# Attention rounds: the third value chunk's transposes, its eviction and the stores of the values moved to the next round's beginning

## The chip, the cores and the metric

The kernel runs on one core of a Trainium2 chip. The metric is the device time of one execution in microseconds (us); lower is better. A core has a matmul engine (TensorE, "PE" in the profile; its weight loads are "PEld"), a vector engine (VectorE, "DVE"), an activation engine (ScalarE, "ACT"), GpSimd ("POOL") and SyncE ("SP"). Each engine works through its own list of instructions in order, and the engines wait for each other by semaphores. DMAs are issued from the lists of SP and of ACT. Matmuls write PSUM, which has 8 banks; the other engines move results from there to SBUF.

## What is computed

The reference is one step of a four-layer decoder trunk for 1024 prompt positions and 8 sample rows, 1032 columns in all. Layer 1 is the one that matters here, differential attention with 8 heads:

```python
q, k, v, g = diff_project(hp, diff_w_in[j], diff_q_gain[j], diff_k_gain[j])
op = diff_output(diff_attend_prompt(q, k, v, lam), g, diff_sub_gain[j], lam_init, diff_w_out[j])
...
    s = jnp.einsum('bthmd,bshmd->bmhts', qb, k).astype(jnp.float32) * scale - slopes[:, None, None] * dist[None]
    s = jnp.where(dist >= 0, s, -jnp.inf)
    p = jax.nn.softmax(s, axis=-1)
    o = jnp.einsum('bmhts,bshv->bmhtv', p, vf)
    return jnp.moveaxis(o[:, 0] - lam * o[:, 1], 1, 2)
```

For the sample rows the same is done against a paged cache of 1024 past positions. The values v of the prompt and of the samples are outputs too (`v_rows_prompt`, `v_cols_sample`), and so are the keys (`k_cols`).

## The kernel before

Activations are held transposed, features by columns, and the 1032 columns are cut into three chunks of 384, 384 and 264 (`CHUNKS`). A weight block of 1024 x 128 is a *unit*; PE multiplies it with one chunk in `unit_chunk`, 8 k-tiles of 3 matmuls each (lines 284 to 286, high and low parts). ACT splits a unit's weights (`split_hi`, line 240) and POOL makes the low part (line 244).

Layer 1 is done in nine *rounds* (`diff_rounds`): round i projects head i (units q, k, v, and the gate g, which belongs to the next round's steps 0 to 2) and does the attention of head i − 1. Round 0 has no attention, round 8 no projection; rounds 1 to 7 are one loop body. On each engine a round is 12 steps s, written out by hand in `body`, and what comes after them. On PE a step puts the first half of a unit chunk (`ks=range(0, KT // 2)`), then attention work, then the second half. The attention works on 8 blocks of 128 query rows: `scores(t)` (line 1283), `probs(tb, half)`, which transposes the probabilities (line 1299), and `values(tb)`, which multiplies them with the values (line 1310). Between them DVE adds the bias and takes the maximum (line 1603), ACT takes exponentials (line 1534), and DVE combines the two softmaxes (lines 1613 to 1616); ACT moves the transposed probabilities to SBUF (line 1473).

Values come out of the projection with features along the partitions and must be turned. `unit_evac` copies a chunk of v from PSUM to `hraw` (line 1458); `value_chunk(x)` on PE transposes its blocks of 128 into a PSUM bank (line 1370); `value_evac(x)` on ACT copies them to `vf` (line 1466) and counts up the semaphore `d_rg`. Chunks 0 and 2 use the same bank (`RG`), and `value_chunk(2)` waits until `d_rg` tells that all evictions before it in the round are done. In the kernel before all this is done in the round of the projection: `value_chunk(0)` in step 10, `value_chunk(1)` in step 11, and behind the steps `value_chunk(2)`, after eight transposes of the finished attention output (line 1416) and ahead of the last small product of the sample rows (line 1423, for a root that ACT makes at lines 1549 and 1551). ACT's end of the round is: two evictions of the attention output (line 1541), `unit_evac(11)`, `value_evac(1)`, `value_evac(2)`, the root, and then DMAs: the attention output (line 1554), the values (lines 1560 and 1562), the keys (line 1565) and the sample output (line 1568). The next round begins on ACT with a load of an activation table (line 1489), `split_hi`, the exponentials of block 0, and the Tanh of the gate's chunk 0 (line 1444), with DVE's product at line 1626. The gate's chunks are stored from ACT's list in steps 2 to 4 (line 1527); the gate's chunk 2 uses chunk 0's buffer and waits for that store (`d_gst`). SP loads slabs of the paged keys and values, 512 KB each (line 1203), as PE frees their slots.

The first scores of a round wait for many things, the last eviction of the values among them:

```python
                    if t == 0:
                        pe.wait_ge(d_qk, done(r.p1.at(0)))
                        pe.wait_ge(d_or, prior(r.p2.at(0)))
                        pe.wait_ge(d_De, prior(r.p2.at(0)))
                        pe.wait_ge(d_rg, done(r.p9.at(8)))
```

`d_rg` counts nine evictions a round: six of the norms of q and k (line 1483) and three of the values, so `p9.at(8)` is the last value eviction of the previous round and `p9.at(7)` the one before it.

Of the kernel before, what the change touches and what calls it, by code (L numbers as in the profile page):

```python
# [15 lines left out]
P = 128  # L16
# [139 lines left out]
def trunk(nc, A, LAYERS=4):  # L156
    ctx = ExitStack()
    with ctx:
# [3 lines left out]
        def sem(name):  # L162
            return ctx.enter_context(nc.semaphore(name))
# [36 lines left out]
        unit_ev = sem("unit_ev")  # L200
# [11 lines left out]
        def ev_val(u, c):  # L212

            return u * NC_ + (c + 1 + CR)
# [375 lines left out]
        def prior(n):  # L590
            return n + 1

        def done(n):
            return n + 2
# [509 lines left out]
        vf = al.take(NBLK, DV)  # L1104
# [19 lines left out]
        wself, vsf, vws, osm, osq2, ors = (al.take(NS) for _ in range(6))  # L1124
# [12 lines left out]
        d_sqd, d_sm, d_rg, d_rq, d_t1 = (sem(x) for x in ("d_sqd", "d_sm", "d_rg", "d_rq", "d_t1"))  # L1137
# [14 lines left out]
        d_kst, d_vst, d_vss, d_sst = sem("d_kst"), sem("d_vst"), sem("d_vss"), sem("d_sst")  # L1152
# [115 lines left out]
        def diff_pe(pe):  # L1268
            def body(r):
                def scores(t):  # L1270
                    if t == 0:
                        pe.wait_ge(d_qk, done(r.p1.at(0)))
                        pe.wait_ge(d_or, prior(r.p2.at(0)))
                        pe.wait_ge(d_De, prior(r.p2.at(0)))
                        pe.wait_ge(d_rg, done(r.p9.at(8)))
                    if t == 4:
                        pe.wait_ge(d_ss, done(r.p1.at(0)))
                    pe.wait_ge(d_mx, prior(r.p16.at(2 * t)))
                    W = (t + 1) * P
                    for a in range(0, W, 512):  # L1280
                        e = min(W, a + 512)
                        for m in range(2):
                            last = nc.tensor.matmul(SSC[m][:, a:e], qf[64 * m:64 * m + 64, t * P:(t + 1) * P],  # L1283
                                                    kf[64 * m:64 * m + 64, a:e], start=True, stop=True)
                            if e == W:
                                last.then_inc(d_sc, 1)
# [16 lines left out]
                def values(tb):  # L1303

                    if r.proj and tb >= 2:
                        pe.wait_ge(d_rg, done(r.n9.at(tb - 2)))
                    pe.wait_ge(d_pe, done(r.p12.at(pidx(tb, tb // 4))))
                    pe.wait_ge(d_on, prior(r.p8.at(tb)))
                    for b in range(tb + 1):
                        last = nc.tensor.matmul(DOB[:, 0:P], pT[tb % 2][:, b, :], vf[:, b, :], start=(b == 0),  # L1310
                                                stop=(b == tb))
                    last.then_inc(d_o, 1)
# [45 lines left out]
                def value_chunk(x):  # L1358

                    c0 = CHUNKS[x][0]  # L1360
                    pe.wait_ge(unit_ev, ev_val(r.unit.at(2), x))
                    pe.wait_ge(d_rg, prior(r.n9.at(6 + x)) if x != 1 else prior(r.n9.at(6)))
                    if r.attn and x == 1:
                        pe.wait_ge(d_mx, done(r.p16.at(15)))
                    if r.attn and x == 0:
                        pe.wait_ge(d_on, done(r.p8.at(7)))
                    for b, w in blocks_of(x):
                        if b < NBLK:
                            o = b * P - c0
                            last = nc.tensor.transpose(VTR[x][:, o:o + P], hraw[:, x % 2, o:o + w], ident[:, :])  # L1370
                    last.then_inc(d_t1, 1)

                for s in range(12):
                    if (s >= 2 * NC_ if r.first else r.proj or s < NC_):
                        unit_chunk(pe, r.unit, s // NC_ - 1, s % NC_, FILL_AT[1], ks=range(0, KT // 2))
                    if r.attn and 3 <= s <= 10:
                        values(s - 3)
                    if r.attn and 2 <= s <= 9:
                        probs(s - 2, 0)
                    if r.attn and s < NBLK:  # L1380
                        scores(s)
                    for b in V_AT.get((s, 0), ()) if r.attn else ():
                        value_row(b)
                    if r.attn and s == 11:
                        pe.wait_ge(d_vo, done(r.p1.at(0)))
                        nc.tensor.matmul(OSB, vo, selv, start=True, stop=True).then_inc(d_vs, 1)
                    if r.attn and 6 <= s <= 9:
                        probs(s - 2, 1)
                    if (s >= 2 * NC_ if r.first else r.proj or s < NC_):
                        unit_chunk(pe, r.unit, s // NC_ - 1, s % NC_, FILL_AT[1], ks=range(KT // 2, KT))  # L1390
                    if r.attn and s in K_AT:
                        key_rows(K_AT[s])
                    if r.attn and s == 3:
                        self_keys()
                    for b in V_AT.get((s, 1), ()) if r.attn else ():
                        value_row(b)
                    if r.attn and s == 5:
                        sample_weights()
                    if r.first and s == 4:
                        pe.wait_ge(d_ld, 16 * 15)  # L1400
                    if r.proj and 4 <= s <= 9:
                        x = s - 4
                        c0, w = CHUNKS[x % NC_]
                        pe.wait_ge(d_sqd, done(r.n6.at(x)))
                        pe.wait_ge(d_rg, prior(r.n9.at(x)))
                        if r.attn:
                            pe.wait_ge(d_on, done(r.p8.at(s - 3)))
                        nc.tensor.matmul(RG[:, 0:w], blk, ss[:, c0:c0 + w], start=True, stop=True).then_inc(d_sm, 1)
                    if r.proj and s >= 10:
                        value_chunk(s - 10)  # L1410
                    if r.attn and s == 11:
                        pe.wait_ge(d_dn, done(r.p1.at(0)))
                        pe.wait_ge(d_pe, done(r.p12.at(11)))
                        for half in range(2):
                            for y in range(4):
                                last = nc.tensor.transpose(DB[half][:, y * P:(y + 1) * P], dall[:, 4 * half + y, :],
                                                           ident[:, :])
                            last.then_inc(d_D, 1)
                if r.proj:
                    value_chunk(2)  # L1420
                if r.attn:
                    pe.wait_ge(d_ssq, done(r.p1.at(0)))
                    nc.tensor.matmul(FSB, ones[:, :], osq2, start=True, stop=True).then_inc(d_F, 1)
# [4 lines left out]
        def diff_act(act):  # L1428
# [5 lines left out]
            def body(r):  # L1434
                i = r.i
# [24 lines left out]
                def value_evac(x):  # L1460
                    c0 = CHUNKS[x][0]
                    nb = 3 if x < 2 else 2
                    act.wait_ge(d_t1, done(r.n3.at(x)))
                    if x == 0:
                        act.wait_ge(d_vst, r.n1.at(0) * 16 + 16)
                    act.activation(vf.rearrange("p b d -> p (b d)")[:, c0:c0 + nb * P], VTR[x][:, 0:nb * P], ACT.Copy)\
                       .then_inc(d_rg, 1)
# [18 lines left out]

                for s in range(12):
                    if r.attn and s == 0:
                        act.preload_act_table_set("exp_and_others")
                    if (s > NC_ if r.first else r.proj or s <= NC_) and s >= 1:  # L1490
                        unit_evac(s - 1)
                    if s == 4:
# [36 lines left out]
                    if r.attn and s < NBLK:  # L1529
                        W = (s + 1) * P  # L1530
                        act.wait_ge(d_nm, done(r.p8.at(s)))
                        for m in range(2):
                            x = (S0[s % 3], S1[s % 2])[m][:, 0:W]
                            act.activation(x, x, ACT.Exp, bias=nm2[:, s % 2, m:m + 1],  # L1534
                                           accum_out=(l8[:, s:s + 1], l1[:, s % 2:s % 2 + 1])[m]).then_inc(d_ex, 1)
                    if r.proj and s == 11:
                        value_evac(0)
# [5 lines left out]
                if r.proj:  # L1543
                    unit_evac(11)
                    value_evac(1)
                    value_evac(2)
                if r.attn:
                    act.wait_ge(d_F, done(r.p1.at(0)))
                    act.activation(ors, FSB, ACT.Ln, bias=eps_t[:, 0:1], scale=1.0 / DV).then_inc(d_or, 1)
# [6 lines left out]
                                      dall[:, 4 * half:4 * half + 4, :].rearrange("p b t -> p (b t)"))\  # L1556
                           .then_inc(d_ost[half], 16)
                if r.proj:
                    act.wait_ge(d_rg, done(r.n9.at(8)))
                    act.dma_start(A["v_rows_prompt"][0, 0, :, bass.ds(i, 1), :]  # L1560
                                  .rearrange("(b p) a d -> p b (a d)", p=P), vf).then_inc(d_vst, 16)
                    act.dma_start(A["v_cols_sample"][bass.ds(i, 1), :, :].rearrange("a d b -> (a d) b"), vsf)\
                       .then_inc(d_vss, 16)
                    act.wait_ge(d_qk, done(r.n1.at(0)))
                    act.dma_start(A["k_cols"][bass.ds(i, 1), :, :].rearrange("a d t -> (a d) t"), kf).then_inc(d_kst, 16)
                if r.attn:
# [522 lines left out]
```

## Time and profile before

| what | value |
|---|---|
| three runs | 3464.18, 3462.76, 3458.08 us (median 3462.76) |
| the profiled execution: its own time | 3459.76 us |
| its span, first to last instruction | 3457.7 us |
| mean granted TensorE clock | 0.973 |
| busy share: PE, PEld, DVE, ACT, POOL | 92%, 82%, 39%, 34%, 15% |
| attention rounds 1 to 7, from one round's first scores to the next's | 91.20 to 93.70 us each |
| DMA | 450.65 MB, mean 130 GB/s |

The profile is of one execution. A busy time counts an engine's instructions, not its waits; ends of matmuls are modelled and matmuls overlap, so a busy PE isn't one at its peak. In the rows below a timeline line gives the start, the time taken, the engine (ACTq and SPq are DMA issues in the lists of ACT and SP), the line of the kernel and the operation with what it writes and reads, and in brackets the idle time of the engine before it and what ended that. Times in us are counted from the span's start.

### The profile page before, as it was taken

The numbers are of one execution on the slowest core, as the hardware profiler recorded it, in microseconds if no ns is written. First come the engines' busy times: TensorE is split into PE (matmuls) and PEld (weight loads), VectorE is DVE, ScalarE is ACT, GpSimd is POOL, SyncE is SP. The second block draws the span as 40 slices with busy tenths as digits, with TensorE's granted clock in tenths as the row PEclk, the third lists the DMA queues.
The fourth block names the chain that finished last, engine by engine and source line by source line (L and its number), as shares of the span: only waits on it lengthen the run. The fifth ranks groups of instructions, "written<-read, shape, count | busy, mean of one in ns | idle before, by whom it ended". The sixth has DMA issues, their size and how long they took to land.

```text
span 3457.7 us, 55121 instructions
## 1 busy us (share of the span) xinstructions
PE 3186.2 (92%) x19786; PEld 2825.5 (82%) x19786; DVE 1354.3 (39%) x3415; ACT 1176.0 (34%) x2293; POOL 523.6 (15%) x224
## 2 busy tenths in 40 slices
PE   6999999997998999999968899979799999999799
PEld 5979697986997777777758788869797979788699
DVE  3231414134434334344345666653524141423531
ACT  3232313232224444444433454531323231323320
POOL 1111020111111101101101122211111101111021
PEclk8999999999999999999989999989899999999999
DMA  6758484757214343444343122131133332424722
GB/s 181 245 156 262 131 244 163 230 186 243 67 37 143 120 137 123 136 137 136 133 144 120 38 60 59 59 113 43 43 120 123 106 129 74 151 87 138 242 76 74
DMA packets 530067, 450.65 MB, mean 130 GB/s; under 512 B 24978, under 2 KB 464658, under 8 KB 529874
## 3 DMA queue, kind: packets, MB, share of 16 engines
q1 hardware_dynamic: 423362, 325.77, 30.4%
q10 hardware_dynamic: 106512, 122.27, 10.2%
q8 instruction: 125, 2.05, 0.2%
q14 instruction: 68, 0.56, 0.0%
HBM read 348.58 MB, written 166.50 MB: 149 GB/s over the span
## 4 chain that ended last, share of the span: by engine, by line
PE 75%; DVE 10%; issue 5%; ACT 4%; DMA 3%; SPq 2%; POOL 1%; ACTq 0%; DVEq 0%; POOLq 0%
PE psum L284 19%; PE psum L285 18%; PE psum L286 18%; PE psum L898 3%; PE psum L894 3%; PE psum L1283 2%; PE psum L1310 2%; DVE Hl L324 2%; DVE hraw L368 2%; PE psum L890 2%; PE psum L873 1%; SPq L393 1%; DMA arena<-scratch_g 1%; POOL Wl L244 1%; PE psum L1353 1%
## 5 line engine op out<-in xcount | busy, mean ns | idle before, releaser
L284 PE MATMUL psum<-Hh,Wh 128*128 128x384 f32 (+1 forms) x4896 | 1646.2, 336 | 163.3 <-DVE Hl L324 64.3
L285 PE MATMUL psum<-Hl,Wh 128*128 128x384 f32 (+1 forms) x4896 | 1583.6, 323 | 0.0
L286 PE MATMUL psum<-Hh,Wl 128*128 128x384 f32 (+1 forms) x4896 | 1582.9, 323 | 0.0
L284 PEld LDWEIGHTS psum<-Hh,Wh 128*128 128x128 f32 x4896 | 938.6, 192 | 236.6 <-issue 99.4
L285 PEld LDWEIGHTS psum<-Hl,Wh 128*128 128x128 f32 x4896 | 940.7, 192 | 6.5 <-issue 0.9
L286 PEld LDWEIGHTS psum<-Hh,Wl 128*128 128x128 f32 x4896 | 938.0, 192 | 0.0
L244 POOL TENSOR_TENSOR Wl<-wraw,Wh 128x1024 fp32r<-128x1024 f32 (+1 forms) x208 | 495.0, 2380 | 2729.4 <-ACT Wh L240 2729.1
L240 ACT ACTIVATE Wh<-wraw 128x1024 fp32r<-128x1024 f32 (+1 forms) x208 | 215.8, 1038 | 339.5 <-PE psum L286 204.6
L419 DVE TENSOR_TENSOR xT<-psum,xT 128x384 f32<-128x384 f32 (+1 forms) x168 | 86.5, 515 | 358.9 <-PE psum L286 358.2
L317 ACT ACTIVATE Hh<-hraw 128x384 fp32r<-128x384 f32 (+1 forms) x252 | 116.2, 488 | 169.3 <-DVE hraw L411 98.7
L953 ACT ACTIVATE hraw<-psum 128x384 f32<-128x384 f32 (+1 forms) x96 | 44.1, 459 | 318.8 <-PE psum L286 318.8
L1052 DVE SCALAR_TENSOR_TENSOR arena<-arena,psum 128x512 f32<-128x512 f32 x56 | 41.9, 748 | 259.2 <-PE psum L898 259.2
L1534 ACT ACTIVATE arena<-arena 128x256 f32<-128x256 f32 (+7 forms) x128 | 98.2, 768 | 116.2 <-DVE arena L1607 116.2
L1074 DVE SCALAR_TENSOR_TENSOR arena<-arena 128x512 f32<-128x512 f32 x128 | 88.9, 747 | 109.7 <-ACT arena L988 109.7
L1040 DVE COPY arena<-psum 128x384 f32<-128x384 f32 (+1 forms) x96 | 48.6, 506 | 212.1 <-PE psum L873 212.1
L993 ACT ACTIVATE arena<-psum,arena 128x512 f32<-128x512 f32 x64 | 44.1, 689 | 248.1 <-DVE arena L574 248.1
L324 DVE TENSOR_TENSOR Hl<-hraw,Hh 128x384 fp32r<-128x384 f32 (+1 forms) x252 | 126.1, 537 | 2.8 <-ACT Hh L317 2.0
L898 PE MATMUL psum<-arena 128*128 128x512 f32 x256 | 120.3, 592 | 0.0
L1603 DVE CUSTOM_DVE_ANT_0 arena<-psum,arena 128x256 f32<-128x256 f32 (+7 forms) x128 | 92.4, 755 | 68.1 <-PE psum L1283 67.4
L1035 DVE TENSOR_SCALAR arena<-psum,arena 128x384 f32<-128x384 f32 (+1 forms) x48 | 27.6, 574 | 226.2 <-PE psum L873 226.2
L894 PE MATMUL psum<-arena 128*128 128x512 f32 x224 | 105.3, 592 | 0.0
L898 PEld LDWEIGHTS psum<-arena 128*128 128x128 f32 x256 | 48.6, 190 | 61.2 <-issue 61.2
(198 smaller groups left out, 2831.7 us busy)
## 6 DMA issues: line engine op xcount, KB each, us to landing
wraw<-in_ret_w_in SPq DMA_DIRECT2D x96, 512.0 KB, 4.2
scratch_kc<-in_cache_kt SPq DMA_DIRECT2D x64, 512.0 KB, 6.1
scratch_vc<-in_cache_vt SPq DMA_DIRECT2D x64, 512.0 KB, 6.7
arena<-in_state_ret ACTq DMA_DIRECT2D x64, 512.0 KB, 6.3
out_ret_state_sample<-arena ACTq DMA_DIRECT2D x64, 512.0 KB, 3.9
arena<-scratch_kc SPq DMA_DIRECT2D x64, 512.0 KB, 4.2
arena<-scratch_vc SPq DMA_DIRECT2D x64, 512.0 KB, 4.3
scratch_on<-arena ACTq DMA_DIRECT2D x80, 256.0 KB, 2.4
```

What stands on the lines that cost most here:

```text
L240: act.activation(Wh[:, j % 2, 0:kt * P], wraw[:, j % 2, 0:kt * P], ACT.Copy).then_inc(w_hi, 1)
L244: pool.tensor_tensor(Wl[:, j % 2, 0:kt * P], wraw[:, j % 2, 0:kt * P], Wh[:, j % 2, 0:kt * P].bitcast(F32), ALU.subtract).then_inc(w_lo, 1)
L284: nc.tensor.matmul(out, hi, xh, start=(k == 0), stop=False)
L285: nc.tensor.matmul(out, hi, xl, start=False, stop=False)
L286: last = nc.tensor.matmul(out, lo, xh, start=False, stop=(k == kt - 1))
L317: act.activation(Hh[:, k, c0:c0 + w], hraw[:, n % HR, 0:w], ACT.Copy).then_inc(h_hi, 1)
L324: nc.vector.tensor_tensor(Hl[:, k, c0:c0 + w], hraw[:, n % HR, 0:w], Hh[:, k, c0:c0 + w].bitcast(F32), ALU.subtract).then_inc(h_lo, 1)
L894: last = nc.tensor.matmul(OB[:, :], qdT[:, r % 2, x, :], St[:, x, :], start=False, stop=(x == 1))
L898: last = nc.tensor.matmul(sbk[:, :], ktok[:, r, x * P:(x + 1) * P], vtok[:, r, :], start=True, stop=True)
L1074: last = nc.vector.scalar_tensor_tensor(sring[:, b % 4, x, :], vbr[:, b % 4, :], kT[:, x, SEQ + b:SEQ + b + 1], sring[:, b % 4, x, :], ALU ...
L1534: act.activation(x, x, ACT.Exp, bias=nm2[:, s % 2, m:m + 1], accum_out=(l8[:, s:s + 1], l1[:, s % 2:s % 2 + 1])[m]).then_inc(d_ex, 1)
L1603: nc.vector.tensor_tensor_reduce(out=(S0[t % 3], S1[t % 2])[m][:, 0:W], in0=SSC[m][:, 0:W], in1=strip[:, SEQ - W:SEQ], scale=1.0, scalar=- ...
```

## The change

The transposes of the values' third chunk move on PE from behind the steps to step 0 of the next round, between the first half of its unit chunk and the scores of block 0. Their eviction on ACT moves to the beginning of the next round, ahead of the table load. The two DMAs that store the values move to step 1 of the next round on ACT, ahead of the first Tanh, and now take the index i − 1. The scores of block 0 wait for the second eviction of values in place of the third; step 3, ahead of the first product with values, waits for the third.

```diff
@@ -1272,7 +1272,7 @@
                         pe.wait_ge(d_qk, done(r.p1.at(0)))
                         pe.wait_ge(d_or, prior(r.p2.at(0)))
                         pe.wait_ge(d_De, prior(r.p2.at(0)))
-                        pe.wait_ge(d_rg, done(r.p9.at(8)))
+                        pe.wait_ge(d_rg, done(r.p9.at(7)))
                     if t == 4:
@@ -1358,8 +1358,12 @@
                 def value_chunk(x):
 
                     c0 = CHUNKS[x][0]
-                    pe.wait_ge(unit_ev, ev_val(r.unit.at(2), x))
-                    pe.wait_ge(d_rg, prior(r.n9.at(6 + x)) if x != 1 else prior(r.n9.at(6)))
+                    if x == 2:
+                        pe.wait_ge(unit_ev, ev_val(r.unit.at(-2), x))
+                        pe.wait_ge(d_rg, prior(r.p9.at(8)))
+                    else:
+                        pe.wait_ge(unit_ev, ev_val(r.unit.at(2), x))
+                        pe.wait_ge(d_rg, prior(r.n9.at(6)))
                     if r.attn and x == 1:
@@ -1373,7 +1377,11 @@
                 for s in range(12):
                     if (s >= 2 * NC_ if r.first else r.proj or s < NC_):
                         unit_chunk(pe, r.unit, s // NC_ - 1, s % NC_, FILL_AT[1], ks=range(0, KT // 2))
+                    if r.attn and s == 0:
+                        value_chunk(2)
                     if r.attn and 3 <= s <= 10:
+                        if s == 3:
+                            pe.wait_ge(d_rg, done(r.p9.at(8)))
                         values(s - 3)
@@ -1416,8 +1424,6 @@
                             last.then_inc(d_D, 1)
-                if r.proj:
-                    value_chunk(2)
                 if r.attn:
                     pe.wait_ge(d_ssq, done(r.p1.at(0)))
@@ -1460,7 +1466,7 @@
                 def value_evac(x):
                     c0 = CHUNKS[x][0]
                     nb = 3 if x < 2 else 2
-                    act.wait_ge(d_t1, done(r.n3.at(x)))
+                    act.wait_ge(d_t1, done(r.p3.at(x) if x == 2 else r.n3.at(x)))
@@ -1486,7 +1492,14 @@
                 for s in range(12):
                     if r.attn and s == 0:
+                        value_evac(2)
                         act.preload_act_table_set("exp_and_others")
+                    if r.attn and s == 1:
+                        act.wait_ge(d_rg, done(r.p9.at(8)))
+                        act.dma_start(A["v_rows_prompt"][0, 0, :, bass.ds(i - 1, 1), :]
+                                      .rearrange("(b p) a d -> p b (a d)", p=P), vf).then_inc(d_vst, 16)
+                        act.dma_start(A["v_cols_sample"][bass.ds(i - 1, 1), :, :].rearrange("a d b -> (a d) b"), vsf)\
+                           .then_inc(d_vss, 16)
@@ -1543,7 +1556,6 @@
                     unit_evac(11)
                     value_evac(1)
-                    value_evac(2)
@@ -1556,11 +1568,6 @@
                 if r.proj:
-                    act.wait_ge(d_rg, done(r.n9.at(8)))
-                    act.dma_start(A["v_rows_prompt"][0, 0, :, bass.ds(i, 1), :]
-                                  .rearrange("(b p) a d -> p b (a d)", p=P), vf).then_inc(d_vst, 16)
-                    act.dma_start(A["v_cols_sample"][bass.ds(i, 1), :, :].rearrange("a d b -> (a d) b"), vsf)\
-                       .then_inc(d_vss, 16)
                     act.wait_ge(d_qk, done(r.n1.at(0)))
```

The lines of the changed kernel stand 4 to 13 further down, so 1370 becomes 1374, 1423 becomes 1429, 1466 becomes 1472 and 1489 becomes 1496. PE's list at the end of the loop body of rounds 1 to 7, before: the transposes of the values' second chunk, eight of the attention output, then those of the third chunk, the sample product and the loop's branch.

```order
L1370 MATMUL psum<-ident,hraw 128x128 x2
L1416 MATMUL psum<-ident,arena 128x128 [waits d_pe,d_dn]
L1416 MATMUL psum<-ident,arena 128x128 x7
L1361 REGISTER_ALU
L1362 REGISTER_ALU [waits unit_ev]
L1370 MATMUL psum<-ident,hraw 128x128 [waits d_rg]
L1370 MATMUL psum<-ident,hraw 128x128
L1423 MATMUL psum<-arena,ones 128x8 [waits d_ssq]
L1185 REGISTER_ALU
L1185 COMPARE_AND_BRANCH
```

In the changed kernel the third chunk's transposes, with their waits for `unit_ev` and `d_rg`, are gone from there:

```order
L1374 MATMUL psum<-ident,hraw 128x128 x2
L1424 MATMUL psum<-ident,arena 128x128 [waits d_pe,d_dn]
L1424 MATMUL psum<-ident,arena 128x128 x7
L1429 MATMUL psum<-arena,ones 128x8 [waits d_ssq]
L1185 REGISTER_ALU
L1185 COMPARE_AND_BRANCH
```

They stand now on PE in step 0 of the next round, between the last matmuls of the unit chunk's first half and the scores of block 0 (line 1283):

```order
L284 MATMUL psum<-Hh,Wh 128x384
L285 MATMUL psum<-Hl,Wh 128x384
L286 MATMUL psum<-Hh,Wl 128x384
L1374 MATMUL psum<-ident,hraw 128x128 [waits d_rg,unit_ev]
L1374 MATMUL psum<-ident,hraw 128x128
L1283 MATMUL psum<-arena 128x128 [waits d_rg,d_De,d_mx,d_or,d_qk]
L1283 MATMUL psum<-arena 128x128
```

Nothing else moved on PE. On ACT the list from the loop's branch into the next pass was, before, the table load, the weights' split, the exponentials of block 0 and the gate's Tanh:

```order
L1185 REGISTER_ALU
L1185 COMPARE_AND_BRANCH
L1489 ACT_TABLE_LOAD
L240 ACTIVATE Wh<-wraw 128x1024 [waits unit_ps,w_loaded0]
L1534 ACTIVATE arena<-arena 128x128 [waits d_nm]
L1534 ACTIVATE arena<-arena 128x128
L1444 ACTIVATE arena<-psum 128x384 [waits d_gst0,unit_ps]
```

Now the eviction (line 1472) stands ahead of the table load, and both stores (lines 1499 and 1501) ahead of the Tanh:

```order
L1185 REGISTER_ALU
L1185 COMPARE_AND_BRANCH
L1472 ACTIVATE arena<-psum 128x256 [waits d_t1]
L1496 ACT_TABLE_LOAD
L240 ACTIVATE Wh<-wraw 128x1024 [waits unit_ps,w_loaded0]
L1547 ACTIVATE arena<-arena 128x128 [waits d_nm]
L1547 ACTIVATE arena<-arena 128x128
L1499 DMA out_v_rows_prompt<-arena 128x8x128 [waits d_rg]
L1501 DMA out_v_cols_sample<-arena 128x8
L1450 ACTIVATE arena<-psum 128x384 [waits d_gst0,unit_ps]
```

At the end of the round ACT's list lost one eviction, ahead of the root, and the two stores, between those of the attention output and of the keys; DVE's, POOL's and SP's lists are as they were.

## Rows read from the trace of the kernel before

**Rows 1.** The page: busy times of the engines, and the chain that ended last.

```profile
PE 3186.2 (92%) x19786; PEld 2825.5 (82%) x19786; DVE 1354.3 (39%) x3415; ACT 1176.0 (34%) x2293; POOL 523.6 (15%) x224
...
PE 75%; DVE 10%; issue 5%; ACT 4%; DMA 3%; SPq 2%; POOL 1%; ACTq 0%; DVEq 0%; POOLq 0%
```

**Rows 2.** PE's waits, 1091 to 1830: engine and line waited for: us in total, times, longest.

```profile
PE psum L1310 <- ACT arena L1483: 20.2, 21, 1.7
...
PE psum L1370 <- ACT arena L1466: 11.5, 7, 1.6
```

**Rows 3.** PE's timeline over one round's end.

```profile
1364.00 1.04 PE L1416 MATMUL psum<-ident,arena 128*128 128x128 f32 x8
1366.68 0.44 PE L1370 MATMUL psum<-ident,hraw 128*128 128x128 f32 x2 [1.65 <-ACT arena L1466]
1366.96 0.29 PE L1423 MATMUL psum<-arena,ones 128*128 128x8 f32 x2
1367.34 0.43 PE L284 MATMUL psum<-Hh,Wh 128*128 128x384 f32 x1
...
1369.61 0.49 PE L1283 MATMUL psum<-arena 64*128 64x128 f32 x4
```

**Rows 4.** PE's timeline at the end of round 0.

```profile
1088.92 0.41 PE L1370 MATMUL psum<-ident,hraw 128*128 128x128 f32 x2 [0.69 <-ACT arena L1466]
```

**Rows 5.** ACT's timeline over the end that rows 3 show.

```profile
1366.12 0.51 ACT L1466 ACTIVATE arena<-psum 128x384 f32<-128x384 f32 x1
1367.16 0.38 ACT L1466 ACTIVATE arena<-psum 128x256 f32<-128x256 f32 x1 [0.53 <-PE psum L1370]
1367.44 0.26 ACT L1549 ACTIVATE arena<-psum,eps_t 128x8 f32<-128x8 f32 x1
1367.74 0.21 ACT L1551 ACTIVATE arena<-arena 128x8 f32<-128x8 f32 x1
...
1368.90 0.39 ACTq L1560 DMA_DIRECT2D out_v_rows_prompt<-arena  x1
...
1370.29 0.53 ACTq L1565 DMA_DIRECT2D out_k_cols<-arena  x1
...
1371.75 1.28 ACT L1489 ACT_TABLE_LOAD   x1 [3.80 <-issue]
...
1374.78 0.47 ACT L1444 ACTIVATE arena<-psum 128x384 f32<-128x384 f32 x1
```

**Rows 6.** ACT's timeline, later in the same round.

```profile
1381.14 0.28 ACT L1473 ACTIVATE arena<-psum 128x128 f32<-128x128 f32 x1 [1.77 <-PE psum L1299]
1381.36 0.38 ACTq L1527 DMA_DIRECT2D scratch_g<-arena  x1
...
1388.37 0.39 ACT L1444 ACTIVATE arena<-psum 128x264 f32<-128x264 f32 x1 [3.72 <-DMA scratch_g<-arena]
```

**Rows 7.** SP's timeline in the same round: the next slabs of keys.

```profile
1379.51 2.30 SPq L1203 DMA_DIRECT2D arena<-scratch_kc  x4
```

**Rows 8.** The tile of the stored values: time from issue to landing.

```profile
DMA to landing us min/median/max: 3.0/3.3/5.0
```

**Rows 9.** Windows: us, busy by engine (count), granted clock, DMA share, GB/s.

```profile
1184.00:1188.00 4.00, 4.00 (x20) 3.34 (x19) 0.77 (x5) 1.90 (x2) 0.00 (x0) 0.72 0.91 303
1376.00:1380.00 4.00, 4.00 (x31) 2.31 (x30) 2.78 (x10) 1.47 (x5) 0.56 (x1) 1.00 0.00 0
1382.00:1388.00 6.00, 6.00 (x37) 5.08 (x37) 1.22 (x5) 1.31 (x4) 0.00 (x0) 1.00 1.02 338
```

**Rows 10.** PE's timeline in the round of rows 3, the transposes of probabilities.

```profile
1394.68 0.52 PE L1299 MATMUL psum<-ident,arena 128*128 128x128 f32 x3 [0.41 <-issue]
```

**Rows 11.** ACT's timeline at the round's other table load.

```profile
1394.36 0.47 ACT L1448 ACTIVATE ss<-psum 128x384 f32<-128x384 f32 x1
1394.85 1.28 ACT L1493 ACT_TABLE_LOAD   x1
1396.14 0.28 ACT L1503 ACTIVATE arena<-psum 128x128 f32<-128x128 f32 x1
```

## Prediction

> **What bounds the kernel now.** I read the page first. TensorE (PE) is busy 92% of the span, VectorE (DVE) 39%, ScalarE (ACT) 34%, and PE also holds three quarters of the chain that ended last [rows 1]. So time is gained where PE stops. The change touches only the stage of the attention rounds, so the second view is PE's waits there [rows 2]: at line 1370, the transposes of values, PE waited 11.5 us in 7 waits, each for an eviction that ACT makes at line 1466; the larger sum, 20.2 us at line 1310, belongs to another place of the round. The third view is PE's timeline over one round's end [rows 3]: eight transposes of line 1416 at 1364.00, then 1.65 us of nothing, then the third value chunk's two transposes at 1366.68, the small product of line 1423, and at 1367.34 the next round's first unit matmul. The same 1.65 us stands at all seven ends of rounds 1 to 7. Round 0, which has no attention, ends with 0.69 us [rows 4].
>
> ACT's timeline over the same end [rows 5] says why: the eviction of chunk 1 starts only at 1366.12 and takes 0.51; PE needs it because the third chunk's bank waits for all earlier evictions of the round. ACT then idles 0.53 for the transposes, evicts chunk 2, issues the stores and comes to its table load at 1371.75.
>
> **The change, part by part.** *The wait.* PE no longer stops behind line 1416: line 1423 needs only a DVE result made during the last unit, and the first half of the next unit needs banks that were free before. By the time that half is done (2.27 us long, 1367.34 to 1369.61 [rows 3]) the eviction of chunk 1 is past: it ends at 1366.63 [rows 5], and PE would come to the transposes at 1369.61 − 1.65 − 0.28 = 1367.68. Gain: 7 × 1.65 + 0.69 = **12.24 us**.
>
> *The two transposes.* They take 0.28 us to the next instruction (1366.68 to 1366.96 [rows 3]) at the old place and, I take it, at the new one. Unknown is the change-over between unit matmuls, transposes and scores: bounded above by the largest change-over of the same view, 1366.96 to 1367.34, 0.38 per round. Bounded below, PE may gain: matmuls overlap, and a PE that doesn't stop starts the next one before the end that is shown for the last. The two transposes are shown 0.44 long and are followed after 0.28, so −0.16. I take 0, since the nearest row is the 0.28 of these same transposes; over 8 boundaries the ends are −1.3 and +3.0.
>
> *The eviction.* ACT loses at the round's end the wait of 0.53, the eviction's 0.28 (1367.16 to 1367.44) and the two issues' 1.39 (1368.90 to 1370.29 [rows 5]), and gets an eviction of 0.38 ahead of the table load: the load comes 0.53 + 0.28 + 1.39 − 0.38 = 1.82 earlier, PE only 1.65. So the exponentials of score block 0 keep pace, and cost nothing.
>
> *The stores.* Both issues now stand behind those exponentials and ahead of the Tanh of the gate's chunk 0. ACT there goes from 1.82 early to 0.43 early, that is 1.22 behind PE's new time. Queued behind are the Tanh of chunk 0, DVE's gate product, its combine of block 0, the maximum of block 1, the next exponentials and the Tanh of chunk 1; that Tanh ends at 1379.37, and ACT then waits 1.77 for PE's transposes [rows 6]. 1.22 fits into 1.77, with 0.55 left. PE's own needs are those transposes of block 0 and, a little before, the bank of the gate's third chunk, which waits only for the first gate product. I cost it at nothing; without this cover it would be up to 1.22 a round.
>
> *The queues.* SP's order is untouched. ACT's queue takes the values' stores some 5 us later. The large one is issued when block 0's exponentials end, 1374.78 − 1.82 = 1373.0 in the new time, and lands 3.3 us later, 5.0 at worst [rows 8]: at 1376.3, at worst with the start of the next large transfers, SP's slabs of keys at 1379.51 − 1.65 = 1377.9 [rows 7]. From 1376 to 1380 nothing moves on the DMA engines at all [rows 9]: that hole takes the store. k's store only moves up.
>
> *The other waits.* They start from PE's scores and move with them; the waits at line 1310 are not touched. The landing of the gate's chunk 0, 1381.36 to 1388.37 [rows 6], is started by PE's own transposes and runs beside SP's slabs, started by PE's own key products; it shifts whole.
>
> The sum against the profiled execution: 3459.76 − 12.24 = 3447.5. That execution lies 3.0 below the median of the three runs; the mean of all four is 3461.2, which gives **3449.0**, my forecast. Behind one of the ends the granted clock fell to 0.72 for 4 us [rows 9], about 4.00 × 0.28 = 1.1 us, which a PE that doesn't stop there may keep.
>
> **The rivals.**
>
> *Slower: the stores meet the slabs.* If the store of 512 KB is still unwritten when SP's four slabs start, it shares the engines' 338 GB/s [rows 9]; at half of that (an estimate, equal shares) it takes 3.1 us, and the gate's chunk 0, behind it in the same queue, lands 3.1 later. ACT's Tanh of chunk 2 waits for that landing (3.72 us now), and through DVE's maximum PE's transposes wait already 0.41 [rows 6, 10], so it goes to PE undiminished: 7 × (3.1 − 1.65) + (3.1 − 0.69) = +12.6, 3473.8. It decides from an issue later than 1377.9 − 3.3 = 1374.6 in the new time; I have 1373.0, so 5%. The Trainium skill ("DMA: Bandwidth & Descriptors", Queues, rings and completion order) speaks against the change here: an engine's completion write lands only after every earlier write from it, so the gate store couldn't report before the values' store is down; no row before shows the two together.
>
> *The table load drains.* In the new order the load stands directly behind an eviction, where before the issues of DMAs stood between. The nearest row says that this is free: at line 1493 a load starts 0.02 after the ACTIVATE before it ends, and 1.28 later work goes on [rows 11]. If it cost one load more, 1.28, ACT would be 2.50 behind against 1.77 of cover: 0.73 of each round's gain goes, leaving 7 × 0.92 − 0.04 = 6.4, 3454.8. The Trainium skill ("ScalarE: Activation LUTs", What ACT_TABLE_LOAD costs) gives 1.38 us of drain with every switch of set; by it the gain would be 5.6 and the time 3455.6. 5%, as the row contradicts it.
>
> *The issues are not absorbed.* If DVE's chain has less cover than ACT's idle time shows, the 1.22 come back: 7 × 0.43 − 0.53 = 2.5 gained, 3458.7. Against it: the 1.77. 6%.
>
> *The wait only moves.* Scores of block 0 wait for the root of line 1551, now ready at 1367.95 − 0.81 = 1367.14; PE would ask at 1367.96. If ACT were a microsecond or two later than I have it, PE would stop there instead and nothing is gained: 3461.2. 3%.
>
> **How the numbers follow.** The forecast has 81%. What a measurement of this kernel can tell from no change is about 0.2%, 6.9 us: the forecast passes it, the three small gains (6.4, 2.5, 0: 14% together) don't, the first rival is slower, 5%. The range: from 3458.08 − 12.24 − 1.3 − 1.1 = 3443.5 to just over the drained table load, 3456; left out are the unabsorbed issues, the moved wait and the slower case, 14%.
>
> **What would show it.** Right: no idle time in front of the third chunk's transposes, now between the unit's first half and the scores; a round 1.6 to 1.8 us shorter; waits at line 1310's place as before (20.2 us in 21); ACT still waiting for PE's transposes behind the Tanh of chunk 1, about 0.5 us; the gate store landing in about 7 us. Wrong: a new wait of PE at the scores of block 0 or at the first transposes of probabilities, a gap between eviction and table load, or a gate store landing in 10 us.

## The result and the profile after

The changed kernel is faster: 3440.56 us in the median of 6 runs (3438.71 to 3442.40) against 3458.14 (6 runs) for the kernel before. The ratio is 0.9946, with a 95% interval of 0.9934 to 0.9958; of 3458 us that is 18.7 us gained (14.5 to 22.8). The forecast was 3449.0 in a range that began at 3443.5, so the sign was right and the size too small. The profiled execution took 3440.44 us with a span of 3437.7, where the one before had 3457.7.

The page shows less PE time and the same work on the other engines as in [rows 1]:

```profile
PE 3180.2 (93%) x19786; PEld 2823.1 (82%) x19786; DVE 1353.7 (39%) x3415; ACT 1175.9 (34%) x2293; POOL 524.1 (15%) x224
```

PE's waits over rounds 1 to 7 (line waited at, releaser, us in total, times, longest) answer to [rows 2]. The 11.5 us at the values' transposes are gone, and line 1374, where these now stand, doesn't wait anywhere. Line 1310 waits as before.

```profile
PE psum L1310 <- ACT arena L1489: 20.1, 21, 1.7
PE psum L1299 <- ACT arena L1479: 4.8, 7, 0.7
PE psum L1299 <- issue: 2.1, 6, 0.7
```

PE's timeline over the same round's end as in [rows 3] (start, us, engine, line):

```profile
1358.15 1.04 PE L1424 MATMUL psum<-ident,arena 128*128 128x128 f32 x8
1359.03 0.29 PE L1429 MATMUL psum<-arena,ones 128*128 128x8 f32 x2
1359.17 0.43 PE L284 MATMUL psum<-Hh,Wh 128*128 128x384 f32 x1
...
1361.36 0.38 PE L1374 MATMUL psum<-ident,hraw 128*128 128x128 f32 x2
1361.67 0.49 PE L1283 MATMUL psum<-arena 64*128 64x128 f32 x4
```

There is no idle time left in it. From the first of the attention output's transposes to the scores of block 0, what I call **the end of a round** below, it takes 1361.67 − 1358.15 = 3.52 us; in [rows 3] it took 1369.61 − 1364.00 = 5.61. So an end gave 2.09 us, not the 1.65 that the old row shows as idle. The steps, each from start to start:

| step | before | after | gain |
|---|---|---|---|
| line 1416/1424 to what follows it | 2.68 | 0.88 | 1.80 |
| sample product to the first unit matmul | 0.38 | 0.14 | 0.24 |
| first half of the unit | 2.27 | 2.19 | 0.08 |
| the values' two transposes | 0.28 | 0.31 | −0.03 |

ACT's timeline over that end answers to [rows 5]:

```profile
1360.28 0.51 ACT L1472 ACTIVATE arena<-psum 128x384 f32<-128x384 f32 x1
...
1363.43 0.38 ACT L1472 ACTIVATE arena<-psum 128x256 f32<-128x256 f32 x1 [2.25 <-issue]
1363.84 1.28 ACT L1496 ACT_TABLE_LOAD   x1
1365.13 1.06 ACT L240 ACTIVATE Wh<-wraw 128x1024 fp32r<-128x1024 f32 x1
1365.37 0.39 ACTq L1499 DMA_DIRECT2D out_v_rows_prompt<-arena  x1
1365.92 0.48 ACTq L1501 DMA_DIRECT2D out_v_cols_sample<-arena  x1
1366.10 0.39 ACT L1547 ACTIVATE arena<-arena 128x128 f32<-128x128 f32 x1
...
1366.86 0.47 ACT L1450 ACTIVATE arena<-psum 128x384 f32<-128x384 f32 x1
...
1373.21 0.28 ACT L1479 ACTIVATE arena<-psum 128x128 f32<-128x128 f32 x1 [1.76 <-PE psum L1299]
1373.43 0.38 ACTq L1540 DMA_DIRECT2D scratch_g<-arena  x1
...
1380.07 0.39 ACT L1450 ACTIVATE arena<-psum 128x264 f32<-128x264 f32 x1 [3.34 <-DMA scratch_g<-arena]
```

Three things are to be seen. The two stores were issued at 1365.37 and 1365.92, while the split of the weights was at work (1365.13, 1.06 long) and ahead of the exponentials (1366.10) that stand before them in the list. The Tanh behind them started 1366.86 − 1361.67 = 5.19 after the scores of block 0; before it was 1374.78 − 1369.61 = 5.17 [rows 3, 5]. And ACT waited 1.76 for PE's transposes, before 1.77 [rows 6]. So the issues cost ACT nothing at all. The time from issue to landing of the values' store:

```profile
DMA to landing us min/median/max: 2.9/2.9/3.0
```

It was down at about 1365.37 + 2.9 = 1368.3, and SP's next slabs were issued at 1371.58.

From one round's first scores to the next's, rounds 1 to 7 took 91.18 to 93.26 us in the trace before (the upper figure of the table ahead of the prediction, 93.70, stands in no row) and take 89.60 to 90.24 now. All seven together took 646.3 and take 629.0: a round is 2.5 us shorter on the mean, not the 1.6 to 1.8 that the prediction named as its sign. The drop of the clock behind one end, 0.95 us, and some time that lies elsewhere in the rounds are in this difference.

### The profile page after: what moved, and what is told of

Same layout as the page of the kernel before. It is cut to its first block, busy times and chain, and to the rows that moved or that the text cites. A ratio compares the mean times of both kernels' runs of the same rounds, so it can differ in the third digit from the quotient of the medians.

```text
span 3437.7 us, 55107 instructions
## 1 busy us (share of the span) xinstructions
PE 3180.2 (93%) x19786; PEld 2823.1 (82%) x19786; DVE 1353.7 (39%) x3415; ACT 1175.9 (34%) x2293; POOL 524.1 (15%) x224
## 4 chain that ended last, share of the span: by engine, by line
PE 76%; DVE 10%; issue 5%; ACT 4%; DMA 3%; SPq 1%; POOL 1%; ACTq 0%; DVEq 0%; POOLq 0%
PE psum L284 19%; PE psum L285 18%; PE psum L286 18%; PE psum L898 3%; PE psum L894 3%; PE psum L1283 2%; PE psum L1310 2%; DVE Hl L324 2%; DVE hraw L368 2%; PE psum L890 2%; PE psum L873 1%; SPq L393 1%; DMA arena<-scratch_g 1%; PE psum L1353 1%; POOL Wl L244 1%
```

## The experiments

Two theories stood against each other. In one, A, all the time comes out of PE's stop at the round's end: its length and what follows it in PE's list. In the other, B, part of it comes from the shorter end of the round on ACT and its DMA queue. For every kernel but that of the last experiment the table gives the ends of rounds 1 to 7, read from PE's timeline; a drop is an end in which the granted clock fell below 1.00, and such ends are left out of the third and fourth column. The first six ends run through the loop's branch, at the seventh the loop falls out.

| kernel | PE's stop | first six ends, us | seventh | drops | time, us (before beside it) | ratio |
|---|---|---|---|---|---|---|
| before | ahead of the branch | 5.61 to 5.63 | 5.36 | 1 | 3458.1 | 1 |
| stores moved alone | ahead of the branch | 5.62 to 5.68 | 5.36 | 2 | 3456.8 (3459.0) | 0.9993 [0.9984, 1.0003] |
| product ahead of the stop | ahead of the branch | 5.60 to 5.61 | 5.26 | 3 | 3459.0 (3459.0) | 0.9996 [0.9986, 1.0005] |
| stop filled | filled with work | 5.62 to 5.69 | 5.35 | 0 | 3456.1 (3459.9) | 0.9988 [0.9979, 0.9997] |
| stop behind the branch | behind it | 5.15 to 5.16 | 5.20 | 0 | 3454.0 (3459.0) | 0.9988 [0.9978, 0.9997] |
| the change | none | 3.51 to 3.52 | 3.52 | 0 | 3440.6 (3458.1) | 0.9946 [0.9934, 0.9958] |
| the change again | none | 3.51 to 3.52 | 3.52 | 0 | 3439.8 (3459.9) | 0.9942 [0.9929, 0.9956] |
| stores at the very beginning | none | 3.52 | 3.52 | 0 | 3441.9 (3459.0) | 0.9945 [0.9927, 0.9962] |

**The stores alone.** The kernel before, with the two stores moved as in the change and the transposes left where they were:

```diff
+                    if r.attn and s == 1:
+                        act.wait_ge(d_rg, done(r.p9.at(8)))
+                        act.dma_start(A["v_rows_prompt"][0, 0, :, bass.ds(i - 1, 1), :]
...
-                    act.wait_ge(d_rg, done(r.n9.at(8)))
-                    act.dma_start(A["v_rows_prompt"][0, 0, :, bass.ds(i, 1), :]
...
```

> The kernel before, with only the two stores of the values moved to step 1 of the next round on ACT; transposes and eviction stay. Theory A (the gain is PE's stop at the round's end, whose whole price from start to start is 2.11 us a round, more than the 1.65 that is shown as idle): PE still stops 1.65 us at every end, a round stays at 92.2 us, the time is within 2 us of the kernel before. Theory B (the stop was worth the 12.2 us shown, and the other 5 us come from ACT's shorter round end and from the quieter DMA queue): rounds some 0.7 us shorter, 4 to 6 us faster.

No gain can be told from noise: 0.9993, with 1 inside the interval. PE's stop is the old one (PE's waits over rounds 1 to 7):

```profile
PE psum L1370 <- ACT arena L1466: 11.5, 7, 1.6
```

The interval reaches to 5.5 us faster, so by the time alone B's lower end, 4, isn't excluded. The trace speaks against it: the seven rounds take 646.2 us, before 646.3, and without the drops (2.8 us here, 0.95 before) 643.5 and 645.4, which is 0.3 a round and not 0.7. Two ends of this trace show a drop, among them the one at 1550 (windows: stretch, us, busy of PE, PEld, DVE, ACT and POOL, granted clock, DMA share, GB/s):

```profile
1550.00:1557.00 7.00, 5.46 (x23) 5.01 (x24) 1.29 (x5) 4.21 (x10) 0.00 (x0) 0.76 0.44 165
```

**The product ahead of the stop.** The kernel before, with the sample product in front of the third chunk's transposes. If the 2.09 contain the shadow of an instruction that merely stood behind the stop, an end gets shorter by it.

```diff
-                if r.proj:
-                    value_chunk(2)
                 if r.attn:
                     pe.wait_ge(d_ssq, done(r.p1.at(0)))
                     nc.tensor.matmul(FSB, ones[:, :], osq2, start=True, stop=True).then_inc(d_F, 1)
+                if r.proj:
+                    value_chunk(2)
```

> The kernel before, with the sample product (line 1423) ahead of the third chunk's transposes, which stay at the round's end. The stop stays but covers one product more: from the attention output's transposes to the next round's first scores 5.62 - 0.28 = 5.34 us, 2 us faster in all. If the loop's branch is exposed behind a stop (theory A's part of 0.24 us), the next unit starts 0.38 us after the transposes, as it did after the product; if those 0.24 us belong to the product and not to the branch, it starts after 0.14, and the end takes 5.10 us.

The ends stayed at 5.60 to 5.61: a miss. PE's timeline at one of them, which also has a drop:

```profile
1276.55 1.04 PE L1416 MATMUL psum<-ident,arena 128*128 128x128 f32 x8
1277.42 0.29 PE L1421 MATMUL psum<-arena,ones 128*128 128x8 f32 x2
1279.23 0.44 PE L1370 MATMUL psum<-ident,hraw 128*128 128x128 f32 x2 [1.52 <-ACT arena L1466]
1279.89 0.61 PE L284 MATMUL psum<-Hh,Wh 128*128 128x384 f32 x1 [0.22 <-issue]
...
1283.73 0.49 PE L1283 MATMUL psum<-arena 64*128 64x128 f32 x4
```

The transposes come as late as ever, 2.68 after line 1416 (an idle time of 1.52 is shown, since the product took 0.13 of the stop). The unit follows them after 1279.89 − 1279.23 = 0.66 us. In [rows 3], with the product between, it was 1367.34 − 1366.68 = 0.66 too. So the product is not what fills these 0.66: in both kernels, behind a stop that is released just ahead of the loop's branch, it takes PE 0.66 from the transposes to the next pass's first matmul, and the product lay in its shadow. The windows of the same end show the drop:

```profile
1275.00:1278.00 3.00, 2.71 (x25) 2.62 (x23) 1.45 (x3) 0.81 (x2) 0.00 (x0) 1.00 0.83 276
1278.00:1284.00 6.00, 4.54 (x18) 4.07 (x18) 0.92 (x2) 1.93 (x7) 0.00 (x0) 0.72 0.50 164
```

From the first unit matmul to the scores it took 1283.73 − 1279.89 = 3.84 us here, and 2.27 at the full clock [rows 3]: 1.57 lost to the clock, behind a stop in which PE did nothing for 1.52. The 0.72 is a mean over a stretch with both levels in it. At the end before this one, whose transposes of line 1416 start at 1183.34, three whole us lie in the drop, at 0.50, the level of 1.2 GHz:

```profile
1188.00:1191.00 3.00, 3.00 (x12) 2.34 (x11) 0.62 (x2) 0.00 (x0) 0.00 (x0) 0.50 1.07 346
```

**The stop behind the branch.** The changed kernel, with the two transposes ahead of the unit's first half instead of behind it. The stop is back, but the branch is past when it comes.

```diff
-                    if (s >= 2 * NC_ if r.first else r.proj or s < NC_):
-                        unit_chunk(pe, r.unit, s // NC_ - 1, s % NC_, FILL_AT[1], ks=range(0, KT // 2))
                     if r.attn and s == 0:
                         value_chunk(2)
+                    if (s >= 2 * NC_ if r.first else r.proj or s < NC_):
+                        unit_chunk(pe, r.unit, s // NC_ - 1, s % NC_, FILL_AT[1], ks=range(0, KT // 2))
```

> The changed kernel, with the third chunk's transposes ahead of the next unit's first half in place of behind it: the branch is passed, but PE stops again. Theory A: from the attention output's transposes to the first scores 2.69 + 0.28 + 2.19 = 5.16 us against 3.51 in the changed kernel and 5.62 before; 3 to 5 us faster than before, the rest of the gain gone. Theory B: the 5 us of the stores and ACT's end stay and the stop comes back: 5 to 7 us faster than before, with the end at 5.6 us.

As expected, an end takes 5.15 to 5.16. PE's timeline:

```profile
1361.85 1.04 PE L1424 MATMUL psum<-ident,arena 128*128 128x128 f32 x8
1362.72 0.29 PE L1429 MATMUL psum<-arena,ones 128*128 128x8 f32 x2
1364.53 0.44 PE L1374 MATMUL psum<-ident,hraw 128*128 128x128 f32 x2 [1.52 <-ACT arena L1472]
1364.73 0.43 PE L284 MATMUL psum<-Hh,Wh 128*128 128x384 f32 x1
...
1367.00 0.49 PE L1283 MATMUL psum<-arena 64*128 64x128 f32 x4
```

The stop is as long as before (2.68 from line 1424), but the unit now follows 0.20 behind the transposes, not 0.66. This cuts the gain of an end into two pieces that experiments tell apart: 5.62 − 5.15 = **0.47 for the branch** behind the stop, and 5.15 − 3.52 = **1.63 for the stop itself**. "The branch" is short for all that PE does between two passes of the loop; what of it takes the time, no run takes apart. The time alone, 4.2 us faster (1.0 to 7.6), fits both theories; the length of the ends does not fit B, and with the trace of the stores alone B falls.

**The stop filled.** The kernel before, with 14 transposes of the identity, whose result nobody reads, put into the stop (bank 6 is free there). If the drops come from PE standing idle, they go, and nothing else changes.

```diff
+                if r.proj and r.attn:
+                    for y in range(14):
+                        nc.tensor.transpose(bank[6][:, (y % 4) * P:(y % 4 + 1) * P], ident[:, :], ident[:, :])
                 if r.proj:
                     value_chunk(2)
```

> The kernel before, with 14 transposes of the identity into a free bank put into PE's stop at each end of rounds 1 to 7 (some 1.5 us of work whose result nothing reads). The stop's end is set by ACT and stays. Theory C (the granted clock drops behind some of the stops, 6 of 21 ends in the three traces that have the stop there, and each drop costs 1.0 to 1.6 us): no drop at the ends of rounds 1 to 7, each end 5.61 us long, 2 to 4 us faster than the kernel before. Rival (the drops are not tied to the stop): one to three drops as in the other three traces, time within 1 us of the kernel before.

PE's timeline, with the new line 1421, and the windows over it:

```profile
1366.51 1.04 PE L1416 MATMUL psum<-ident,arena 128*128 128x128 f32 x8
1367.39 1.69 PE L1421 MATMUL psum<-ident 128*128 128x128 f32 x14
1369.19 0.44 PE L1370 MATMUL psum<-ident,hraw 128*128 128x128 f32 x2
...
1369.86 0.44 PE L284 MATMUL psum<-Hh,Wh 128*128 128x384 f32 x1
...
1372.14 0.49 PE L1283 MATMUL psum<-arena 64*128 64x128 f32 x4
```

```profile
1364.00:1374.00 10.00, 9.78 (x73) 9.09 (x72) 4.10 (x11) 2.75 (x8) 0.00 (x0) 1.00 0.63 201
```

The ends are as long as before, 5.62 to 5.69, but none of the seven shows a drop, and the kernel is 0.9988 [0.9979, 0.9997] of the time before: 4.2 us (1.0 to 7.3) for work that nobody needs. By C's 2 to 4 us that is as expected; the rival had it within 1 us.

**The stores at the very beginning.** The changed kernel, with both stores issued in step 0 behind the eviction, ahead of the table load. It takes back the cover that the exponentials give them.

```diff
                         value_evac(2)
-                        act.preload_act_table_set("exp_and_others")
-                    if r.attn and s == 1:
                         act.wait_ge(d_rg, done(r.p9.at(8)))
...
+                        act.preload_act_table_set("exp_and_others")
```

> The changed kernel, with the two stores in step 0 directly behind the eviction and ahead of the table load in place of step 1. Table load, split and exponentials come about 1.1 us later. If issues are absorbed (ACT waits 1.76 us for PE later in the round): time as the changed kernel, 15 to 18 us faster than before. If they are not: 1.0 us a round lost, 7 to 10 us faster than before.

The time is that of the change, 0.9945 against 0.9946. ACT's timeline:

```profile
1367.06 0.39 ACTq L1497 DMA_DIRECT2D out_v_rows_prompt<-arena  x1
1367.61 0.48 ACTq L1499 DMA_DIRECT2D out_v_cols_sample<-arena  x1
1368.12 1.28 ACT L1501 ACT_TABLE_LOAD   x1 [1.23 <-issue]
...
1371.15 0.47 ACT L1450 ACTIVATE arena<-psum 128x384 f32<-128x384 f32 x1
...
1376.29 0.28 ACT L1479 ACTIVATE arena<-psum 128x128 f32<-128x128 f32 x1 [0.55 <-PE psum L1299]
```

Here the first issue waits for the eviction right before it (its end, 1366.51 + 0.38), so no activation is queued ahead of the issues when they are made, and they do hold ACT up: 1.23 idle, and the Tanh starts 6.41 behind the scores (which start at 1364.74) instead of 5.19. ACT's wait for PE's transposes shrinks from 1.76 to 0.55, and PE notices nothing. This is the very case that the prediction had costed for the change itself, 1.22 behind with 0.55 left.

**The change again**, unaltered, as the base of the next one on the same chip.

> The changed kernel once more, beside the next one. Theory: ends of 3.52 us in all seven rounds, no drop of the clock there, 15 to 20 us faster than the kernel before.

3439.81, 0.9942 [0.9929, 0.9956]; ends of 3.51 to 3.52.

**The roots earlier.** The larger wait of [rows 2], at line 1310, lies in the middle of the round: the products with values wait for the logarithms of two norm chunks, which stand on ACT behind the exponentials of blocks 6 and 7 (line 1489 in the waits of the change). In the changed kernel I put these two logarithms ahead of the step's exponentials, and left the rest of the roots in place.

```diff
+        EARLY = (2, 3)
...
+                    if x not in EARLY:
+                        root_ln(x)
...
+                    if r.proj and s - 4 in EARLY:
+                        root_ln(s - 4)
                     if r.attn and s < NBLK:
```

> The changed kernel, with ACT's logarithms of the norms' chunks 2 and 3 ahead of the exponentials of blocks 6 and 7 in place of behind them. PE's waits for them (0.78 and 1.68 us a round, shown at the products with values) should go. If a stop costs more than is shown (0.17 us for matmuls that had run out): 7 x 2.46 to 7 x 2.8, 17 to 20 us faster than the changed kernel. Rival: the exponentials come 0.6 to 0.8 us later, and PE waits for what hangs on them (transposes of probabilities in steps 8 and 9): only 8 to 12 us faster than the changed kernel.

It took 3424.85 us (3421.29 to 3427.60), 0.9900 [0.9885, 0.9915] of the kernel before, and 15.0 less than the change beside it. That lies between the two expectations, 17 to 20 and 8 to 12, and meets neither. PE's waits over rounds 1 to 7:

```profile
PE psum L1299 <- ACT arena L1481: 7.7, 14, 0.7
PE psum L1310 <- ACT arena L1491: 2.9, 7, 0.4
PE psum L1299 <- issue: 1.2, 3, 0.5
```

Line 1310's wait fell from 20.1 to 2.9, that is by 17.2, and 2.9 of it came back at the transposes of probabilities, whose wait rose from 4.8 to 7.7. A round takes 87.2 on the mean (610.56 / 7) against 89.7 in the trace of the change again (627.70 / 7). That is 17.1 us in seven rounds; why the time shows 2 us less isn't traced. This version beats both kernels.

## Why the prediction was right or wrong

**What bounds the kernel: right.** The time was won where PE stops. The stores moved alone gave nothing that can be told from noise.

**The gain, 7 × 1.65 + 0.69 = 12.24: the step that failed.** As a price of the stop itself it holds. Between the kernel with its stop behind the branch and the change, the seven ends differ by 36.13 − 24.62 = 11.5; round 0's end, from chunk 1's transposes to the scores, takes 3.61 in the one and 2.73 in the other, 0.9; together 12.4. These are the first and the last row of round 0's end in the kernel before (3.91), with the stop behind the branch, and with the change:

```profile
1087.73 0.49 PE L1370 MATMUL psum<-ident,hraw 128*128 128x128 f32 x3
1091.64 0.49 PE L1283 MATMUL psum<-arena 64*128 64x128 f32 x4
...
1088.49 0.49 PE L1374 MATMUL psum<-ident,hraw 128*128 128x128 f32 x3
1092.10 0.49 PE L1283 MATMUL psum<-arena 64*128 64x128 f32 x4
...
1089.02 0.49 PE L1374 MATMUL psum<-ident,hraw 128*128 128x128 f32 x3
1091.75 0.49 PE L1283 MATMUL psum<-arena 64*128 64x128 f32 x4
```

What failed is taking it for the whole price. Two things stood behind the stop:

- *The branch.* The loop's branch was hidden as long as PE's list ran ahead, and lay open behind the released stop. Six ends of 0.47, the seventh of 5.36 − 5.20 = 0.16 and round 0 with 3.91 − 3.61 = 0.30 make 3.3. The prediction had the row for it, the 0.38 between product and unit matmul [rows 3], and used it as the upper bound of a *cost* of the change-overs. It was a part of the stop's price: 0.14 is left of it.
- *The clock.* The prediction named the drop of [rows 9] and allowed 1.1 us for it at the low end only, as a thing that had happened once. It recurs: in the three traces with an idle stop ahead of the branch 6 of 21 ends have one, and those ends are longer by 0.95, 1.22, 1.57, 0.95, 1.57 and 1.55, or 7.81 / 3 = 2.6 for an execution. This is an estimate from three traces, and rather low: it counts up to the first scores, and behind the first end of the kernel before, whose scores start at 1184.90, the clock was still down [rows 9]. In the four traces without the stop it is 0 of 28. That the idle PE is the cause is made likely by this and by the filled stop, which shows none in 7 and gains about that much, but it is not shown: the stop behind the branch shows none in 7 either, though PE idles there just as long. At 6 of 21, seven ends without a drop come about by chance in one of ten traces, so whether the place matters stays open.

The sum is 12.4 + 3.3 + 2.6 = 18.3, measured 18.7 (14.5 to 22.8). That the two lie so close is in part luck, by the width of the interval. The seven rounds' sums bear it out more sharply: 646.3, 646.2 and 646.6 us in the three traces with an idle stop ahead of the branch, 643.3 with the stop filled, 639.6 with it behind the branch, and 629.0, 627.7 and 628.4 in the change, its repetition and the stores at the very beginning. That is 18.0 between the first and the last group, and 1.2 of round 0 come on top, where the sum above has 17.1 and 1.2; the 0.9 left over is not traced.

**The base.** The forecast started from 3461.2, the mean of four times; beside the changed kernel the one before had a median of 3458.14. These 3.1, the 3.4 by which the ends gave more than 12.24 (15.64 together) and the 2.6 of the clock make 9.1; the forecast was 8.4 too high.

**Change-overs taken at 0, between −1.3 and +3.0.** The transposes at their new place have 0.31 to the next instruction for 0.28: right. The lower bound was too narrow for the reason above.

**The eviction: right.** Counted from line 1416's (now 1424's) transposes, the table load starts 5.69 behind them where it started 7.75 behind [rows 3, 5]: 2.06 earlier, PE 2.09. The exponentials keep pace, as forecast; of the 2.06 the working had 1.82, and no run takes the rest apart.

**The stores at nothing: the right figure for the wrong reason.** The working had ACT 1.22 late and 0.55 of its wait left. In fact ACT is not late, and its wait is the old one, 1.76: these issues were made ahead of activations that are still queued, and cost the engine time in the kernel where none were. The 1.39 of [rows 5] had stood where none were either, behind the round's last activation. An engine's list is thus not worked strictly in its order where DMA issues stand in it. The cover was there all the same, as the kernel with the stores at the beginning shows: 1.2 late, 0.55 left, no loss.

**The queues: right.** The store was issued 3.70 behind the first scores where the working had 5.0, and landed 3 us ahead of SP's slabs. The hole of [rows 9], 1376 to 1380, was read in the old time; in the forecast's new time it lies 1.65 earlier, which changes nothing. The gate's store lands after 6.6 us (1373.43 to 1380.07), and the Tanh waits 3.34 for it where it waited 3.72 [rows 6]. The rival in which stores and slabs meet did not come about; what it would have cost, no run here shows. Nor does one show the rule that the prediction has beside it from the Trainium skill ("DMA: Bandwidth & Descriptors", Queues, rings and completion order).

**The table load: right.** It starts 0.03 behind the eviction (1363.43 + 0.38 to 1363.84) and the split starts right behind its 1.28. The Trainium skill ("ScalarE: Activation LUTs", What ACT_TABLE_LOAD costs) has 1.38 us of drain with every switch of set. This order of instructions shows none, and the measurement decides.

**The other waits: right.** Line 1310 waits 20.1 in 21, before 20.2 in 21, and no new wait at the scores appeared. Of the three smaller gains none took place.

## What to carry to other kernels

Price a stop from start to start, from the last instruction ahead of it to the first one that runs at its usual pace behind it, and not by the idle time that the row shows: what follows a stop in the list, a loop's branch above all, loses its cover, and the clock may fall. Work of the next pass that already has its inputs was the best filling here, 18.7 us against 4.2 for useless transposes, and a stop at a loop's end deserves it before an equal one elsewhere, since here the branch's 0.47 came on top. When one stop is gone, list the remaining ones by total and treat the largest the same way; here the next one gave 15 us more for two instructions moved.

## What the runs showed of the hardware that was not expected

- When a wait right ahead of the loop's branch is released, it takes PE 0.66 us from the two released transposes to the next pass's first matmul, with or without the sample product between. With the same wait behind the branch the next matmul follows these transposes after 0.20, and where PE's list had run ahead the next pass's first matmul follows the sample product after 0.14.
- Behind a stop of about 1.6 us the granted clock can fall from the level of 2.4 GHz (1.00) to that of 1.2 GHz (0.50): it did at 6 of 21 ends, 0.72 as the mean over 6 us, with up to 1.57 us lost before the scores. Fourteen useless transposes in the stop were no slower than an idle PE, and by the interval faster (1.0 to 7.3 us).
- A DMA issue in ACT's list was made at 1365.37, ahead of exponentials that stand before it in the list and started at 1366.10. Its 0.39 cost the engine nothing there; ahead of the table load, behind a wait for the eviction just before, two issues left it idle for 1.23.
